# Final normalisation of the mixture-of-experts output: from a phase of its own into the expert steps

## The reference, cut to what matters

```python
m, ... = hybrid_mixer(x, ...)                # projections, convolutions, RG-LRU, W_out
x = layer_norm(ALPHA * x + m, ln1_g, ln1_b)
x = layer_norm(ALPHA * x + hier_moe(x, ...), ln2_g, ln2_b)

def hier_moe(x, ...):                        # 4 groups of 4 experts, top 1 group, top 2 experts in it
    ...
    h = silu(einsum('nd,edf->nef', xt, moe_w1)) * einsum('nd,edf->nef', xt, moe_w3)
    h = h * gates[..., None]
    return einsum('nef,efd->nd', h, moe_w2)  # each token: the sum of its two experts' rows
```

## Time and profile before

| | us |
|---|---|
| median of 3 runs (1301.26 to 1305.11) | 1303.81 |
| the profiled execution, whole | 1298.67 |
| its span, first to last instruction | 1296.6 |
| PE busy | 1140.4 (88%) |
| DVE busy | 782.8 (60%) |
| ACT busy | 503.3 (39%) |
| POOL busy | 153.0 (12%) |

### The profile page before, as it was taken

One profiled execution on the slowest core, in us unless ns is written; L12 is line 12 of the kernel. 1 busy time (PEld: TensorE's weight loads), 2 busy tenths in 40 slices (PEclk: granted clock), 3 DMA queues, 4 the chain that ended last, 5 costly groups with the idle time before them and its releaser, 6 DMA issues. The chain is left out here.

```text
span 1296.6 us, 20522 instructions
## 1 busy us (share of the span) xinstructions
PE 1140.4 (88%) x5818; PEld 1028.6 (79%) x5819; DVE 782.8 (60%) x1476; ACT 503.3 (39%) x650; POOL 153.0 (12%) x192
## 2 busy tenths in 40 slices
PE   6999999999999999999999757999999999996000
PEld 6999999999999997888887655888888888875000
DVE  5666554644564565665665664566666666632898
ACT  4554443633543453222222224455555554421000
POOL 1000000000000010023322250000000000000720
PEclk9999999999999999999999877999999999998555
DMA  5432565275430055154433166667667776522972
GB/s 182 134 93 67 131 130 104 82 145 105 78 105 20 21 158 170 66 163 163 162 131 84 67 188 239 201 252 276 231 240 278 280 250 221 198 99 92 407 287 101
DMA packets 82772, 207.39 MB, mean 160 GB/s; under 512 B 18064, under 2 KB 44720, under 8 KB 76464
## 3 DMA queue, kind: packets, MB, share of 16 engines
q0 software_dynamic: 21984, 100.53, 21.7%
q1 hardware_dynamic: 53840, 89.63, 20.6%
q10 hardware_dynamic: 6912, 16.79, 7.5%
HBM read 133.99 MB, written 72.93 MB: 160 GB/s over the span
## 5 line engine op out<-in xcount | busy, mean ns | idle before, releaser
L1227 PE MATMUL ps_h<-w_hi,xt_hi 128*128 x336 | 136.4, 406 | 0.0
L1227 PE MATMUL ps_h<-w_lo,xt_hi 128*128 x336 | 132.4, 394 | 0.0
L1227 PE MATMUL ps_h<-w_hi,xt_lo 128*128 x336 | 132.3, 394 | 0.0
L277 PE MATMUL ps_vb_c<-x_hi,w_hi 128*128 (+1 forms) x320 | 113.9, 356 | 11.2 <-DVE x_lo L441 11.2
L277 PE MATMUL ps_vb_c<-x_hi,w_lo 128*128 (+1 forms) x320 | 113.3, 354 | 0.0
L277 PE MATMUL ps_va_b<-x_hi,w_lo 128*128 (+1 forms) x320 | 112.7, 352 | 0.0
L277 PE MATMUL ps_vb_c<-x_lo,w_hi 128*128 (+1 forms) x320 | 112.6, 352 | 0.0
L277 PE MATMUL ps_va_b<-x_hi,w_hi 128*128 (+1 forms) x320 | 112.6, 352 | 0.0
L277 PE MATMUL ps_va_b<-x_lo,w_hi 128*128 (+1 forms) x320 | 111.8, 349 | 0.0
L1321 DVE TENSOR_TENSOR w_lo_p<-ps_o,w_hi_p 128x512 f32<-128x512 f32 x84 | 54.0, 685 | 54.4 <-PE ps_o L1211 54.4
L1018 DVE TENSOR_TENSOR w_lo<-w_raw,w_hi 128x2048 f32 (+1 forms) x32 | 73.1, 2287 | 11.8 <-ACT w_hi L1013 11.8
(11 more groups left out here) (260 smaller groups left out, 2580.6 us busy)
## 6 DMA issues: line engine op xcount, KB each, us to landing
w_raw<-in_w POOLq DMA_DIRECT2D x48, 1024.0 KB, 6.0
w_lo_p<-xs_scr SPq DMA_DIRECT2D x43, 512.0 KB, 4.7
o_scr<-w_lo_p SPq DMA_DIRECT2D x42, 512.0 KB, 2.7
w_raw<-in_w_in POOLq DMA_DIRECT2D x19, 512.0 KB, 3.6
x_raw<-in_x_t SPq DMA_DIRECT2D x20, 416.0 KB, 3.4
xs_scr<-x_raw ACTq DMA_DIRECT2D x16, 512.0 KB, 7.0
o_scr<-x_raw ACTq DMA_DIRECT2D x16, 512.0 KB, 8.4
x_hi_p<-y_scr SPq DMA_DIRECT2D x16, 512.0 KB, 4.5
```

The source lines that it names most:

```text
L277: mm = pe.matmul(ps[i][:, 0:CHUNK], w[:, i, k], x[:, k, bass.ds(c * CHUNK, CHUNK)], start=(k == 0 and n == 0), stop=(k == KT - 1 and n == 2))
L1227: mm = pe.matmul(ps_h[par][:], x[:, par, k], w[:, bass.ds(at, 1), k].rearrange("p o n -> p (o n)"), start=(k == 0 and n == 0), stop=(k == ...
```

## The change

`finish_phase` goes, and its work is done inside the expert steps.

- **Ranked tiles.** `later_experts` and `ranks` (some 23 small DVE instructions and two matmuls, ahead of the first step) order the tokens by the later of their two experts. Tile 0 has the first 32 of them, the other 16 tiles have 128 each. For each token a record of three integers (its row in the output, its two rows in `o_scr`) is put at its rank, by 17 indirect DMAs of POOL in step 0, and read back by SP (`order`).
- **Pairs of steps.** `slots` and `count_pairs` find how many pairs are needed so that no tile is gathered before its rows are stored. `steps` now unrolls the first four steps, loops from pair 2 with a constant bound of 16, then emits 13 pairs that carry tiles: one pair without, ten with one tile each (`pair`), and four single steps with one tile each. The normalising pass of tile 13 and all of tiles 14, 15 and 16 come after the last step.
- **A tile's way in a pair.** POOL gathers it in the odd step before (`fetch`); DVE sums it and takes its statistics at the end of the even step (`fin_sum`); ACT takes the root at the end of that step and then runs a one-column Silu (`root`, `idle`); DVE finishes it at the end of the odd step (`fin_norm`); POOL scatters it to the output (`put`). There are two buffers `v` and one `v1`.
- **POOL by steps.** Its weight loads are now called from its own `step`, behind `fetch` and `put`.
- **Zero fills.** The fills of `o_scr` rise from 2 to 5 in each of 8 chunks: 9 DMAs in place of 6.

In the diff, `tiles` is the triple (gather, sum, normalise), and `early(s, n)` is true for steps known to be below n.

```diff
+FLAST = 2
+FPAIR = NT - 3 - 2 * FLAST
+FTAIL = FPAIR + FLAST + 1
+OFILL, STORED = 5, 8
+PLAN = 2 * ((STEPS - NT) // 2 + 1 + FTAIL)
...
+            for i in range(OFILL):
+                act.dma_start(o_scr[bass.ds((q * OFILL + i + STORED) * P, P), :], zero).then_inc(s_zo, 16)
...
-        def steps(eng, emit):
+        def steps(eng, emit, ready=None):
             eng.wait_ge(s_plan, 1)
-            pairs = eng.value_load(plan[0:1, 0, STEPS + 1:STEPS + 2], min_val=0, max_val=(STEPS - NE) // 2) + NE // 2
-            emit(0, 0, 0, 2)
-            emit(1, 1, 0, 2)
-            with eng.Fori(1, STEPS // 2 - 1) as h:
-                with eng.If(h < pairs - 1):
-                    emit(h * 2, 0, h, 2)
-                    emit(h * 2 + 1, 1, h, 2)
-            emit(pairs * 2 - 2, 0, pairs - 1, 1)
-            emit(pairs * 2 - 1, 1, pairs - 1, 0)
+            for s in range(4):
+                emit(s, s % 2, s // 2, 2, None)
+            eng.wait_ge(s_pairs, 1)
+            pairs = eng.value_load(planned[0:1, 0:1], min_val=0, max_val=PLAN // 2 - FTAIL - 2) + (FTAIL + 2)
+            with eng.Fori(2, PLAN // 2 - FTAIL) as h:
+                with eng.If(h < pairs - FTAIL):
+                    emit(h * 2, 0, h, 2, None)
+                    emit(h * 2 + 1, 1, h, 2, None)
+            if ready:
+                ready()
+            def pair(f, b, h):
+                emit(h * 2, 0, h, 2, (None, (f, b), None))
+                emit(h * 2 + 1, 1, h, 2, ((f + 1, 1 - b), None, (f, b)))
+            h = pairs - FTAIL
+            emit(h * 2, 0, h, 2, None)
+            emit(h * 2 + 1, 1, h, 2, ((0, 0), None, None))
+            for f in range(2):
+                pair(f, f, pairs - (FTAIL - 1 - f))
+            with eng.Fori(0, (FPAIR - 2) // 2) as i:
+                for n in range(2):
+                    pair(i * 2 + (2 + n), n, i * 2 + (pairs - (FTAIL - 3 - n)))
+            tile = lambda f: (f, f % 2)
+            for n in range(2 * FLAST):
+                f = FPAIR + n
+                emit(pairs * 2 - (2 * FLAST - n), n % 2, pairs - (FLAST - n // 2), min(2, 2 * FLAST - 1 - n),
+                     (tile(f + 1), tile(f), tile(f - 1) if n else None))
             return pairs * 2 - 1, pairs - 1
...
+            def fetch(f, b, stored):
+                summed, free, copied = (count(pool, n) for n in (f, f * 16 - 16, f + 1))
+                if early(f, 1):
+                    pool.wait_ge(s_fin, 16)
+                else:
+                    pool.wait_ge(s_sum, 1)
+                    pool.wait_ge(s_sum, summed)
+                if not early(f, 2):
+                    pool.wait_ge(s_y, 16)
+                    pool.wait_ge(s_y, free)
+                pool.tensor_copy(id_f[:, b], fin[:, bass.ds(f, 1)].rearrange("p o n -> p (o n)")).then_inc(s_idf, 1)
...
+                for c, to in enumerate((v[b], v1)):
+                    pool.indirect_dma_start(to, None, o_scr[0:STEPS * P],
+                                            bass.IndirectOffsetOnAxis(id_f[:, b, 1 + c:2 + c], 0)).then_inc(s_v, 16)
+            def put(f, b):
+                n = TAIL if early(f, 1) else P
+                done, before = count(pool, f + 1), count(pool, f * 16)
+                pool.wait_ge(s_fn, 1)
+                pool.wait_ge(s_fn, done)
+                if not early(f, 1):
+                    pool.wait_ge(s_y, 16)
+                    pool.wait_ge(s_y, before)
+                pool.indirect_dma_start(y_out, bass.IndirectOffsetOnAxis(id_f[0:n, b, 0:1], 0),
+                                        v[b][0:n], None).then_inc(s_y, 16)
...
+            def step(s, par, h, left, tiles):
+                if tiles:
+                    get, add, norm = tiles
+                    stored = (h, h - 1) if par == 0 else (h, h)
+                    if get and not (add and norm):
+                        fetch(*get, stored)
+                    if norm:
+                        put(*norm)
+                    if get and add and norm:
+                        fetch(*get, stored)
+                more = pool.value_load(plan[0:1, 3, bass.ds(s, 1)], min_val=0, max_val=1)
+                with pool.If(more):
+                    weights(pool.value_load(plan[0:1, 0, bass.ds(s, 1)], min_val=0, max_val=NE - 3) + 2)
...
+            _, pair = steps(pool, step)
+            put(NT - 4, (NT - 4) % 2)
+            fetch(NT - 2, (NT - 2) % 2, (pair + 1, pair))
+            put(NT - 3, (NT - 3) % 2)
+            fetch(NT - 1, (NT - 1) % 2, (pair + 1, pair + 1))
+            put(NT - 2, (NT - 2) % 2)
+            put(NT - 1, (NT - 1) % 2)
+            pool.wait_ge(s_y, 16 * NT)
...
+            def root(f, b):
+                act.wait_ge(s_mv, f + 1)
+                act.activation(std[:, b:b + 1], mv[:, b, 1:2], ACT.Sqrt, bias=eps[:]).then_inc(s_std, 1)
...
                     ew.hi2(act, expert + 1, at)
+                if tiles and tiles[1]:
+                    root(*tiles[1])
+                    if left:
+                        act.activation(idle[:], eps[:], ACT.Silu)
                 act.wait_ge(s_sil, 1)
...
                 with dve.If(split):
                     ew.lo2(dve, expert + 1, at)
+                if tiles:
+                    _, add, norm = tiles
+                    if norm:
+                        fin_norm(*norm)
+                    if add:
+                        fin_sum(*add)
+                if isinstance(s, int) and s == 1:
+                    count_pairs()
                 dve.wait_ge(s_hid, 1)
                 dve.wait_ge(s_hid, s + 1)
+            def fin_sum(f, b):
+                n = TAIL if early(f, 1) else P
+                dve.wait_ge(s_v, f * 32 + 32)
+                dve.tensor_tensor(v[b][0:n], v[b][0:n], v1[0:n], ALU.add).then_inc(s_sum, 1)
+                dve.wait_ge(s_sum, f + 1)
+                for c in range(2):
+                    ins = dve.bn_stats(stats[0:n, c], v[b][0:n, c * 512:c * 512 + 512])
+                ins.then_inc(s_bn, 1)
+                dve.bn_aggr(mv[0:n, b], stats[0:n]).then_inc(s_mv, 1)
+            def fin_norm(f, b):
+                n = TAIL if early(f, 1) else P
+                dve.wait_ge(s_std, f + 1)
+                dve.reciprocal(rstd[0:n, b:b + 1], std[0:n, b:b + 1]).then_inc(s_rstd, 1)
+                dve.scalar_tensor_tensor(out=v[b][0:n], in0=v[b][0:n], scalar=mv[0:n, b, 0:1], in1=ln2[0:n, 0],
+                                         op0=ALU.subtract, op1=ALU.mult).then_inc(s_fx, 1)
+                dve.wait_ge(s_rstd, f + 1)
+                dve.wait_ge(s_fx, f + 1)
+                dve.scalar_tensor_tensor(out=v[b][0:n], in0=v[b][0:n], scalar=rstd[0:n, b:b + 1], in1=ln2[0:n, 1],
+                                         op0=ALU.mult, op1=ALU.add).then_inc(s_fn, 1)
...
+            ranks()
             x_lo(0, 0)
             slots()
...
             last, pair = steps(dve, step)
             h_lo(last)
+            fin_norm(NT - 4, (NT - 4) % 2)
+            fin_sum(NT - 3, (NT - 3) % 2)
             evict(last, 1, pair)
-def finish_phase(nc, o_scr, y_out, wreg, ln, sfin):
...
+            for f in (NT - 3, NT - 2):
+                fin_norm(f, f % 2)
+                fin_sum(f + 1, (f + 1) % 2)
+            fin_norm(NT - 1, (NT - 1) % 2)
...
```

More of the change, by code:

```diff
@@ L1060, in moe_phase @@
         scol = sb("scol", [P, 8])
-        vals = sb("vals", [P, 3])
-        pairs = sb("pairs", [1, 2], I32)
+        vals = sb("vals", [P, 4])
+        pairs = sb("pairs", [1, 2])
         big = sb("big", [P, NT, NE])
         slf = sb("slf", [P, TOPK, NT])
+        ln2 = sb("ln2_sb", [P, 2, D])
+        v = [rows(wreg[i], 4, 5)[:, 0] for i in (2, 3)]
+        v1 = x_raw[:].rearrange("p a b c -> p (a b c)")[:, 0:D]
+        last_e = sb("last_e", [P, NT])
+        later, rank = sb("later", [P, NT, NE]), big
+        tot2, inc2 = (v[0][:, i * NT * NE:(i + 1) * NT * NE].rearrange("p (e t) -> p e t", e=NE) for i in range(2))
+        fin_e = sb("fin_e", [P, 2, NE])
+        fcol = sb("fcol", [P, 4, NT])
+        fint = sb("fint", [P, 4, NT], I32)
+        need = sb("need", [P, 1])
+        rec = sb("fin_rec", [P, NT, 3], I32)
+        fin = sb("fin", [P, NT, 3], I32)
+        id_f = sb("id_f", [P, 2, 3], I32)
+        stats = sb("stats2", [P, 2, 6])
+        mv = sb("mv2", [P, 2, 2])
+        std, rstd = sb("std2", [P, 2]), sb("rstd2", [P, 2])
+        eps, idle = sb("eps2", [P, 1]), sb("idle", [P, 1])
         ps_x = ctx.enter_context(nc.psum_tensor("ps_x", [P, KT, P], F32))
@@ L1149, in _ @@
             load_gate(2, 0, 1, load(2, 0))
-            last, _ = steps(sp, step)
+            last, _ = steps(sp, step, order)
             store(last, 1)
@@ L1190, in _ @@
             weights(1)
-            with pool.Fori(2, NE) as e:
-                weights(e)
+            def fetch(f, b, stored):
[9 more added lines that the diff above has]
+                pool.tensor_copy(id_f[:, b], fin[:, bass.ds(f, 1)].rearrange("p o n -> p (o n)")).then_inc(s_idf, 1)
+                for par in range(2):
```

(35 more changed lines are left out.)

175 lines of the change are left out of this document (85 added, 90 removed).

## The result

The changed kernel takes **1356.99 us**, median of 4 runs (1351.96 to 1359.28), against 1304.46 (1301.26 to 1305.48) for the kernel before. The ratio is 1.0402, 95% interval 1.0367 to 1.0436. The prediction had the direction (slower) and missed the size: 1312, range 1280 to 1334. The profiled execution took 1357.4 us with a span of 1355.7; before these were 1298.7 and 1296.6.

A forecast was written before the change was run, and what follows sets the result against it. PE was taken to bound the expert steps and DVE the tail; -67.5 tail, +56 waits, +3 loop, +15 clock and +1.5 start gave +8 on 1303.8, so 1312 us, range 1280 to 1334.

The forecast's parts named there:

- the tail: After the last step's T: 45 us left in place of 112.6, a saving of 67.5 us (63 to 79).
- the skip: Tile loop's skipped iterations, eight instead of three: +3 us (1 to 6).
- the waits: Tile steps: PE waits ahead of output for work held by sums, root and passes, +56 us (49 to 66).
- the clock: Tile steps: PE's clock falls after waits, 2 us a time, two thirds of 22 taken: +15 us (0 to 28).
- the third part, a late second split: Steps 28 and 34: second split and the work behind it end late, 2.7 of the 7 us put on each.
- at nothing: Extra fills, covered by ACT's 6.0 us wait for PE, and step 0's 17 scatters, 21 us of POOL: no cost.
- the start behind the router: Ahead of step 1: some ten more instructions in slots delay it, +1.5 us (0 to 4).
- (b): Rival, tile steps: weights come late behind gathers and puts on POOL's queue, +20 us, 1332; chance 0.12.
- a tail over 55: Sign: the forecast is wrong if last T to the end, put at 45 us, takes over 55.
- (a): Rival, tile steps: the clock holds and its 15 us go, 1297; chance 0.25.
- (c): Rival, ACT in tile steps: switching tables costs more than its load; at twice as long, +17 us, 1329; chance 0.06.
- (d): Rival, tile steps: they hide all the moved work, ACT's hold included, 1246; chance 0.10.

The follow-up runs named there:

- experiment 4: Changed kernel with ACT's root and one-column Silu moved from the end of the sum's step to behind the next step's Silu: ratio 1.0295.
- 7: Kernel of experiment 4 with DVE's sum of a tile also moved, to the next step behind h_lo and x_lo: ratio 1.0169.
- experiment 9: Kernel of 7 with POOL no longer waiting for one weight slice to land before issuing the next: ratio 0.9976.
- 2: Changed kernel with 16 of the 24 additional zero fills moved out of the mixer's groups 1 and 2: ratio 1.0347.
- experiment 3: Changed kernel with the 17 scatters of records moved from step 0 into the loop, behind POOL's steps 4 and 5: ratio 1.0393.
- experiment 5: Changed kernel with records of 64 bytes instead of 12, same 17 scatters in the same place: ratio 1.0435.
- experiment 6: Changed kernel with POOL waiting, after every third of the 17 scatters, until all so far have landed: ratio 1.0351.
- Experiment 8: Changed kernel with the loop of plain pairs ending at 11 instead of 16, skipping three iterations instead of eight: ratio 1.0366.
- Experiment 10: Changed kernel with its last put as a plain SP store to other tokens' rows instead of POOL's scatter: ratio 1.0347.
- experiment 12: Changed kernel with fills moved, scatters in threes, root and sum moved, tail reordered, and weight loads not paced: ratio 0.9808.
- 1: Kernel before with only the extra fills, five of o_scr instead of two in each of eight mixer chunks: ratio 1.0045.

## Why the prediction was right and wrong

The direction came out as forecast, and the sum was 51 us short: the start lacks 16.4, steps 0 to 5 lack 15.4, the tail 12.3, the skip 3.8, the rest 3.3. In the tile steps two errors nearly cancel, which is luck: the waits were put at 56 and are 39.4, under the lower bound of 49, and the clock was put at 15 and is 28.5, at the end of its bounds (0 to 28).

**Right: what holds the steps.** ACT's root ahead of `h_hi`, with a start of `output` at T+10.7 in a split step (10.8 measured). The stretch lost 70.8 us against 69. But that is right only as a sum (3 us of it lie in the last step). PE waited 39.4 us more than before, not 56. In the six split steps it waited 3.4 to 3.7 (4.1 and 4.6 predicted: with the waits a step is longer, and PE reaches its output later than T+6.6); steps 28 and 34 cost 0.7 and 2.7 each, not 7, since the third part, a late second split, was hidden; steps without a split cost 0.7 (1.0), steps 39 and 40 took 3.2 and 4.0 (3.6 each). From step 20 to 28 the Silus are 14.3 to 15.2 and 10.4 to 11.7 us apart in turn, where 14 to 16 and 9.5 were forecast.

**Wrong: the clock, 28.5 instead of 15.** Four traces give PE's idling and its extra busy time between Silus 17 and 41: 41.1 and 28.5 (changed kernel), 31.8 and 17.7 (experiment 4), 20.3 and 12.4 (7), 12.7 and 8.2 (9). The changed kernel's trace is the dearest of its kind: with the same tile steps, experiments 2, 3, 5, 6, 8 and 10 show 23.0 to 26.1 for 41.4 to 43.5 us of idling. Each us waited costs another 0.56 to 0.69; over the changed kernel's ten waits above 2.5 us it is 2.9 each, against 2 in the prediction, which let only two thirds of them count. The Trainium skill's TensorE: Matmul & The Clock Gate, section on HAM oscillation, has a loop with recurring waits pay in every round. The traces agree with the rule, and the prediction should have followed it: the price of one wait was in the earlier trace rows, and the chain of waits only had to be counted in full.

**Wrong: "at nothing", the 17 scatters.** The prediction asked only whom POOL's 21 us keep from their weights. They keep every engine from issuing: +15.4 us in steps 0 to 5. Experiment 6 takes that away and pays part of it back in late weights; 12 takes it away for good. The rows of eight scatters in the trace of before do no harm. The one longer row, twelve ahead of the first step, holds an issue of 7.33 us where the others take about 1, the only hint that a longer row is another matter:

```profile
765.69 7.33 POOL L764 DMA_INDIRECT g_scr<-r_wts,r_sli  x1 [0.30 <-issue]
```

Seventeen scatters in a row stand nowhere in it, and the cost should have had an upper bound like any other unseen operation.

**Wrong: "at nothing", the fills.** ACT's 6.0 us of cover is time on ACT's queue. What the fills use up is the 16 DMA engines, whose share is in the page's slices and was not read there. The stores of `yb` land late, and ACT waits for their buffer (its pass that writes `yb`, from 150 to 360 us):

```profile
its engine sat idle before it (us, times) until:
  DMA y_scr<-yb: 23.1, 5
```

Most of that wait is covered: PE idles 7.5 us from 150 to 360, where before it idled none, at a DMA share of 0.94 (0.53 before). By experiments 1 and 2 the fills cost 6 to 7 us.

The other 11 of the start's 17.9 have three parts. About 4 remain in the mixer, where the stall of the fills itself differs (the last gelu starts at 495.2 to 501.8 with the full fills). From there to DVE's write of `plan`, which ends the router, are 275.8 us before and 278.5 in the changed kernel, and 272.2 to 278.5 over all traces: 2.7 is within the spread of that stage, and what picks the value stays open. The third part, 4.8, lies behind the router.

**Wrong: the start behind the router, 4.8 instead of 1.5.** From `plan` to Silu 0 are 31.9 us before and 36.7 after. Silu 0 waits there for expert 1's weights. POOL issues their first slice when the first two x tiles have landed, 20.5 us behind `plan` (17.2 before), and the second only when the first slice has landed; ACT's split waits for the second:

```profile
805.30 0.57 POOL L1225 DMA_DIRECT2D w_raw<-in_w  x1 [5.92 <-DMA w_raw<-in_w]
...
811.83 1.91 ACT L1021 ACTIVATE w_hi<-w_raw 128x2048 f32 x1 [5.03 <-DMA w_raw<-in_w]
```

The ten traces of the changed order with loads paced like this have 36.7 to 38.9 us from `plan` to Silu 0. The two without the pacing, experiments 9 and 12, have 33.2 and 33.0 with all of the new work in them, 1.1 to 1.3 over before and near the 1.5 allowed. So the term that failed is (b)'s, late weights, in the one place where it was not looked for. The x tiles are loaded some 4 us later than before because the router's last scatters land later; why they do was not followed up.

**Under-sized: the skip.** The measured +8.3 less before's 1.9 is 6.4, where +3 (1 to 6) stood. Experiment 8 shows what was left out: 3.7 us are PE's waiting (5.45 - 1.71), and the rest of its 6.2 is slower matmuls behind that wait.

**Mis-sized: the tail, 57.4 instead of 45.** The sum of tile 14 ended at T+21.3 (19 predicted), of 15 at T+31.3 (28), the last pass at T+43.6 (40); tile 16's gathers were issued at T+31.0 (26.5), since they also waited for the put of tile 14, issued behind that tile's pass (T+25.3) and landed at T+29.9. Then 13.8 us to the end where the prediction had 4, by the stores' landing. Experiment 10 shows that this is POOL's own end, a DRAIN of 9.3 us behind the landing of its last put. By the prediction's own sign, a tail over 55, the forecast is wrong here.

**The rivals.** (b), late weights, was given 0.12 and did not show in the changed kernel's tile steps, which were too slow for it; it showed ahead of Silu 0 only. It was there all the same, the next bound under the first (experiments 7 and 9). (a) and (c) are out: the granted clock fell to 0.92, and no load took more than its 1.28 us. (d) was wrong for this order of work, but a better order comes near it: experiment 12 loses 19 us between Silus 17 and 41 (243.7 against 224.5).

## What to carry to other kernels

Work moved from a tail into a dense loop must be priced on every queue it passes and not only by engine time: here ACT's order, then DVE's, then POOL's were each the bound, one hidden under the other. With all three mended the change broke even (0.9976), and it paid (0.9808) with the fills, the scatters and the tail mended as well. A cost put at nothing needs the resource that really hides it (the DMA engines' share, not the issuing engine's idle time), and an operation that no trace shows in such a row needs an upper bound. A wait that recurs on PE costs about 0.6 us more for each us waited, since the clock falls behind it (0.56 to 0.69 in four kernels here).

## What the runs showed of the hardware

- The row of 17 scatters of records, 1.27 us apart on POOL, stops the issue of ACT, DVE, PE and SP some 5 us after its start. The idling of ACT is 13.6 us (changed kernel), 12.8 (experiment 3) and 19.9 (experiment 5), with 12 or 64 bytes a record alike. With a wait for landing behind every third nobody stops (experiment 6). The router's rows of eight scatters stop nobody either; what makes the difference stays open.
- In the twelve kernels with puts, the span ends 12.05 to 12.25 us after the issue of POOL's last put: 2.3 to 2.6 us to landing, then a DRAIN of POOL of 9.2 to 9.3 us.
- Zero fills drive the DMA share to 0.94 to 1.15 at 155 to 186 GB/s, while weights, gathers and stores together move 270 GB/s at 0.77 (experiment 9's window).
- A Silu starts 0.01 us behind a table load of 1.28 us in every switch of the tile steps. The Trainium skill, ScalarE: Activation LUTs, on what ACT_TABLE_LOAD costs, adds a drain of 1380 ns; the trace does not show it.
